# Inputs of a two-layer diffusion trunk laid out on the host: feature-major x, condition and vectors, weights in contiguous chunks

## The chip, the cores and the metric

The kernel runs on one core of a Trainium2 chip. The metric is the device time of one execution in microseconds (us); the median of three runs is shown. All data is f32.

## The reference, cut to what matters

The program runs two layers over two groups of tokens: 512 latent tokens (x_sample, conditioned by c) and 128 context tokens (x_prompt, conditioned by c_ctx). D_MODEL is 1024. What the change touches is the head of each layer:

```python
mod = (jax.nn.silu(cond) @ lw['w_ada'] + lw['b_ada'])[:, None, :]
sh1, sc1, gt1, sh2, sc2, gt2 = jnp.split(mod, 6, axis=-1)
h = rmsnorm(x, lw['g_norm1']) * (1.0 + sc1) + sh1
(qa, ka, va, qb, kb, vb, zb, ab, bb, qc, kc, vc, ga, gb, gc) = split_cols(h @ lw['w_in'])
```

w_ada is 1024 x 6144 and w_in 1024 x 8208 for each layer. The short convolution of the DeltaNet branch reads conv_w, its decays read the 16 columns ab and bb of w_in, and the expert router reads w_router. After the branches and the output projection comes the expert-choice mixture of 16 experts, which reads 96 chunks of 2 MB in each layer.

## The kernel before, in words

x is held in SBUF feature-major as xT, 128 partitions x 8 blocks k x 640 tokens (512 latent, then 128 context). h is held in the same way as hT. Weights pass through a ring of three slots of 2 MB (four in the expert stage). SyncE (SP) issues their loads in the order of PLAN: for a layer first the w_ada chunks 0 to 3, then the w_in chunks qb, kb, vb, zb, then the rest of w_ada and w_in mixed, the branch and output weights, and the experts (`load_plan`, the DMA itself in `load`). `slot_free` lets SP issue the load of a chunk once the chunk that was three before it has been used. A w_ada or w_in chunk is 512 columns of all 1024 rows, so a partition takes 8 pieces of 2 KB from 8 rows of the matrix. PE takes the chunks in the same order.

Start of the program. ScalarE (ACT) issues two loads of x as it lies, tokens on partitions, into xtok. GpSimd (POOL) issues the first constants, then c and c_ctx as 8 rows of 128 each into crow, then ten small loads of layer vectors into vrow, one row for each 128 values. PE turns crow (L1071), and DVE copies the result into ccol, padded with zeros, which is the stationary side of the w_ada matmuls. PE turns x_prompt (L1077) and x_sample (L1082) through PSUM, eight blocks of five tiles, and ACT copies each block out to xT (L1579, L1582) and squares it (L1598); DVE adds the squares (L2000). Between the blocks PE does the matmuls of w_ada chunk 0 (after block 3) and chunk 1 (after block 6), L957. Then PE sums the squares over the partitions (L1053 to L1057), does chunks 2 and 3, turns the vectors (L972), and folds the modulation (L966). ACT takes the root, DVE the reciprocal (L1991) and the vectors (L2011), ACT copies the modulation out (L1587, L1591), and DVE and ACT make hT block by block: `norm_scale` (L2006) and `shift` (L1619). The projection of qb starts on the context columns (L933, 64 matmuls; its first eight wait for a block of hT each) and goes on with the latent columns (L943). SP issues w_ada chunk 3 after chunk 0 is used, qb after chunk 1, kb after chunk 2, and vb after chunk 3.

Turn of the layers. After the experts PE does w_ada chunk 0 of the next layer (L957), then adds up the experts' output and turns it back to feature-major (L1528 to L1537) from ysum, which POOL loads from DRAM (L901, five loads of 512 KB), with w_ada chunks 1 to 3 between the blocks and the turn of the vectors after block 6. POOL issues the ten vector loads and the small loads (a_log, dt_bias, lam_qk, the 16 columns ab of w_in as wab, w_router) right behind the ysum loads.

Of the kernel before, what the change touches and what calls it, by code (L numbers as in the profile page):

```python
# [106 lines left out]
LAYER_CHUNKS = PRE_CHUNKS + NMOE  # L107
FIRST_UNITS = KD + 2

# [47 lines left out]
def wo_unit(l, half, m):  # L157

    return unit_no(l, "wo") + (8 + half if m is None else 4 * half + m)


def x_unit(k):
    return 2 + k

# [205 lines left out]
def build(nc, A, O):  # L370
    with ExitStack() as ctx:
# [32 lines left out]
        def at(off, shape):  # L404
            n = int(np.prod(shape))
            v = arena[:, off:off + n]
            if len(shape) == 2:
                v = v.rearrange("p (a b) -> p a b", a=shape[0])
            if len(shape) == 3:
                v = v.rearrange("p (a b c) -> p a b c", a=shape[0], b=shape[1])  # L410
            return v
# [68 lines left out]
        iota, onehot = at(9856, (T,)), at(9216, (T,))  # L480
        xtok = at(0, (NT, D))
        gates, gatep = at(15104, (512,)), at(15616, (256,))
        xrow = hT.rearrange("p k t -> p (k t)").rearrange("p (t d) -> p t d", t=NT)
        frow = at(10496, (D,))
        ysq = at(NS, (D,))
        crow = at(5120, (P,))

# [19 lines left out]
        def tile_t(t):  # L507
            return slice(t * P, (t + 1) * P)
# [49 lines left out]
        def _(sp):  # L558
# [8 lines left out]
            def load(c, src, words=4096, n=512):  # L567
                slot_free(c)
                s = slot_of(c)[0]
                sp.dma_start(ring[s][:, 0:words].rearrange("p (k n) -> p k n", n=n), src)\  # L570
                    .then_inc(sig[f"chunk{s}_loaded"], 16)

            for l in range(DEPTH):
                win = A["w_in"][l].rearrange("(k p) n -> p k n", p=P)

                def load_plan(q):
                    name, i = PLAN[q]
                    c = chunk_no(l, name, i)
                    if name == "ada":
                        load(c, A["w_ada"][l].rearrange("(k p) n -> p k n", p=P)[:, :, 512 * i:512 * i + 512])  # L580
                    elif name == "wo":
                        load(c, A["w_out"][l].rearrange("(k p) n -> p k n", p=P)[:, :, 512 * i:512 * i + 512])
                    elif name.startswith("br"):
                        load(c, A["w_br_" + name[2]][l].rearrange("(k p) n -> p k n", p=P)[:, :, 512 * i:512 * i + 512],
                             2048)
                    else:
                        load(c, win[:, :, SEG[name] + 512 * i:SEG[name] + 512 * i + 512])

# [117 lines left out]
        def _(pool):  # L706
            first = CST["tri"][0]
            pool.dma_start(cst[:, 0:first], A["consts"][:, 0:first]).then_inc(sig["consts_loaded"], 16)
            for i, n in enumerate(("c", "c_ctx")):
                src = A[n][0] if n == "c" else A[n]  # L710
                pool.dma_start(crow[8 * i:8 * i + 8, :], src.rearrange("(k p) -> k p", p=P))\
                    .then_inc(sig["cond_loaded"], 16)
            for l in range(DEPTH):

                if l:
                    pool.wait_ge(sig["logits_rowed"], 2 * l)
                rows = [(V_BADA, 48, A["b_ada"][l].rearrange("(m p) -> m p", p=P)),
                        (V_G1, 8, A["g_norm1"][l].rearrange("(m p) -> m p", p=P)),
                        (V_G2, 8, A["g_norm2"][l].rearrange("(m p) -> m p", p=P)),
                        (V_GO, 1, A["g_onorm"][l:l + 1, :]), (V_GS, 1, A["g_subln"][l:l + 1, :])]  # L720
                for r, n, src in rows:
                    pool.dma_start(vrow[r:r + n, :], src).then_inc(sig["vectors_loaded"], 16)
                for j in range(CONV):
                    pool.dma_start(vrow[V_CONV + 12 * j:V_CONV + 12 * j + 12, :],
                                   A["conv_w"][l, j].rearrange("(c p) -> c p", p=P)).then_inc(sig["vectors_loaded"], 16)
                if l == 0:
# [7 lines left out]
                    .then_inc(sig["small_loaded"], 16)  # L734
                pool.dma_start(wab, A["w_in"][l].rearrange("(k p) n -> p k n", p=P)[:, :, SEG["ab"]:SEG["ab"] + 16])\
                    .then_inc(sig["small_loaded"], 16)
                pool.dma_start(wrt, A["w_router"][l].rearrange("(k p) n -> p k n", p=P)).then_inc(sig["small_loaded"], 16)

# [44 lines left out]

                pool.wait_ge(sig["vectors_turned"], l + 1)
                pool.memset(rpt, 0.0).then_inc(sig["rows_cleared"], 1)
# [119 lines left out]
        def _(pe):  # L905
# [63 lines left out]

            def turn_vectors(l):  # L970
                pe.wait_ge(sig["vectors_loaded"], 160 * (l + 1))
                tr(W[3 if l else 2][:, 0:V_ROWS], vrow[0:V_ROWS, :], ident[0:V_ROWS, 0:V_ROWS])\  # L972
                    .then_inc(sig["vectors_turned"], 1)

            def modulate(l, a):
                for _ in ada(l, a):
                    pass
# [90 lines left out]
            pe.wait_ge(sig["consts_loaded"], 16)  # L1068
            pe.wait_ge(sig["cond_silu"], 1)
            pe.wait_ge(sig["cond_loaded"], 32)  # L1070
            tr(W[0][:, 0:16], crow[0:16, :], ident[0:16, 0:16]).then_inc(sig["cond_turned"], 1)  # L1071
            pe.wait_ge(sig["cond_ready"], 1)
            pe.wait_ge(sig["x_loaded"], 32)
            for half in range(2):
                big = begin(half)
                for k in range(4):
                    last = tr(big[:, tile_t(k)], xtok[:, NTS, tile_t(4 * half + k)], ident)  # L1077
                used(last)
            for k in range(KD):
                big = begin(x_unit(k))  # L1080
                for t in range(NTS):
                    last = tr(big[:, tile_t(t)], xtok[:, t, tile_t(k)], ident)  # L1082
                used(last)
                if k in (3, 6):
                    modulate(0, k // 4)
            norm_sum(0)
            modulate(0, 2)

            for l in range(DEPTH):
                if l == 0:  # L1090
                    modulate(0, 3)
                    turn_vectors(0)
                    for _ in fold(0, 3):
                        pass
# [437 lines left out]
                for k in range(KD):  # L1532
                    if k >= 1:
                        pe.wait_ge(sig["x_added"], XADDS * (l + 1) - KD + k - 1)
                    mm(W[2 + 2 * (k % 2)][:, :], final[:, tile_t(k)], onehot[0:SL, 0:TS], start=True, stop=False)
                    for t in range(NTS):
                        last = mm(W[2 + 2 * (k % 2)][:, tile_t(t)], ysum[t][:, tile_t(k)], ident,  # L1537
                                  start=False, stop=t == NTS - 1)
                    last.then_inc(sig["sum_turned"], 1)
                    if k in (1, 3, 5):  # L1540
                        modulate(l + 1, (k + 1) // 2)
                    if k == 6:
                        turn_vectors(l + 1)
                norm_sum(2 * l + 2)
# [17 lines left out]
        def _(act):  # L1562
# [3 lines left out]

            act.dma_start(xtok[:, 0:NTS, :], A["x_sample"][0].rearrange("(t p) d -> p t d", p=P))\
                .then_inc(sig["x_loaded"], 16)
            act.dma_start(xtok[:, NTS, :], A["x_prompt"][0]).then_inc(sig["x_loaded"], 16)

# [50 lines left out]

            act.wait_ge(sig["cond_loaded"], 32)
            a_(crow[0:16, :], crow[0:16, :], ACT.Silu).then_inc(sig["cond_silu"], 1)
            for half in range(2):
                copy_context(half, xT[:, 4 * half:4 * half + 4, TS:T])
            for k in range(KD):
                copy_unit(x_unit(k), xT[:, k, 0:TS])
                act.wait_ge(sig["unit_emptied"], x_unit(k) + 1)
                square(0, k)
# [347 lines left out]
        def _(dve):  # L1977
# [31 lines left out]
            def keep_vectors(l):  # L2009
                dve.wait_ge(sig["vectors_turned"], l + 1)  # L2010
                ch.link(v_.tensor_copy(vcol[:, :], W[3 if l else 2][:, 0:V_ROWS]))  # L2011

            v_.memset(ones[:, :], 1.0)
            v_.memset(small[:, 528:544], 0.0)
            v_.memset(W[5], 0.0)
            ch.link(v_.memset(ccol[:, :], 0.0))
            dve.wait_ge(sig["cond_turned"], 1)
            for g in range(2):
                last = v_.tensor_copy(ccol[:, 0:8 * KD].rearrange("p (k c) -> p k c", c=8)[:, :, 6 + g], W[0][:, KD * g:KD * g + KD])
            last.then_inc(sig["cond_ready"], 1)  # L2020
            dve.wait_ge(sig["consts_loaded"], 16)
# [500 lines left out]

            dve.wait_ge(sig["vectors_loaded"], 160 * DEPTH + 16)
            dve.wait_ge(sig["scattered"], 16 * SUMS * DEPTH)
# [14 lines left out]


# [15 lines left out]
```

## Time and profile before

| | us |
|---|---|
| median of 3 runs (lowest, highest) | 3163.93 (3163.28, 3166.62) |
| the profiled execution | 3165.57 |
| its span in the profile | 3163.8 |
| PE busy | 3071.8 (97%) |
| DVE busy | 1240.3 (39%) |
| ACT busy | 612.5 (19%) |
| POOL busy | 243.2 (8%) |

The span is cut into 40 slices of 79 us in the page's strips. PE is at nine tenths in nearly all of them; the DMA strip stands at nine tenths in two blocks of slices, which are the expert stages of the two layers, and between two and seven tenths elsewhere. Every time below is in us from the start of the span. The profiled execution lies 1.64 us above the median, and 1.8 us of it are outside the span.

### The profile page before, as it was taken

How to read it: one execution, taken by the hardware profiler on the slowest of the kernel's cores; microseconds unless marked ns; L12 is line 12 of the kernel's file. 1: busy time of each engine (PE TensorE's matmuls, PEld its weight loads, DVE VectorE, ACT ScalarE, POOL GpSimd, SP SyncE). 2: the span in 40 equal slices, each digit the busy share in tenths (PEclk: the TensorE clock that was granted, in tenths of full speed). 3: DMA queues.
4: the chain of work that ended last, by engine and by line, in shares of the span. 5: the costliest groups of instructions: out<-in, count | busy, mean ns of one | idle time of the engine just before them, and what ended most of it. 6: DMA issues, size and time to landing. Idle time of an engine off the chain costs nothing.

```text
span 3163.8 us, 43528 instructions
## 1 busy us (share of the span) xinstructions
PE 3071.8 (97%) x18861; PEld 1628.3 (51%) x18861; DVE 1240.3 (39%) x2402; ACT 612.5 (19%) x1358; POOL 243.2 (8%) x391
## 2 busy tenths in 40 slices
PE   7999999999998999999999999999999989999998
PEld 4555565656556444444355546665565464443433
DVE  4459553364343121121154694432644331121113
ACT  3141001143423000000022400011534230000001
POOL 1011000011001000000100100001110010000000
PEclk9999999999999999999999999999999989999999
DMA  7346543522333999999961573544224259999997
GB/s 243 110 127 187 151 140 98 162 92 72 130 126 128 347 393 388 394 391 387 386 194 61 176 193 96 150 140 123 79 72 157 97 179 369 394 395 389 391 390 291
DMA packets 227135, 695.17 MB, mean 220 GB/s; under 512 B 12210, under 2 KB 25750, under 8 KB 223616
## 3 DMA queue, kind: packets, MB, share of 16 engines
q1 hardware_dynamic: 199200, 613.97, 54.9%
q0 software_dynamic: 21312, 62.80, 6.8%
q10 hardware_dynamic: 6432, 15.62, 1.3%
q8 instruction: 149, 2.44, 0.3%
q14 instruction: 42, 0.34, 0.0%
HBM read 618.66 MB, written 73.68 MB: 219 GB/s over the span
## 4 chain that ended last, share of the span: by engine, by line
PE 91%; DMA 5%; ACT 2%; DVE 1%; issue 0%; SPq 0%; ACTq 0%; DVEq 0%
PE unit L994 14%; PE unit L1480 13%; PE unit L943 12%; PE work L1483 10%; PE work L1480 6%; PE unit L1006 4%; PE unit L985 4%; PE unit L1025 4%; PE unit L1352 3%; PE unit L933 3%; DMA ring<-in_w_e_gate 2%; PE unit L1305 1%; PE work L1173 1%; PE work L957 1%; PE unit L1364 1%; PE work L1196 1%
## 5 line engine op out<-in xcount | busy, mean ns | idle before, releaser
L994 PE MATMUL unit<-hT,ring 128*128 128x512 f32 x1024 | 452.6, 594 | 0.0
L1480 PE MATMUL unit<-ring,arena 128*64 128x512 f32 x1568 | 356.1, 600 | 5.3 <-DMA ring<-in_w_e_gate 3.9
L994 PEld LDWEIGHTS unit<-hT,ring 128*128 128x128 f32 x1024 | 189.4, 190 | 217.7 <-issue 217.7
L2486 DVE SCALAR_TENSOR_TENSOR arena<-work,arena 32x256 f32<-32x256 f32 x128 | 61.6, 482 | 552.1 <-PE work L1483 550.7
L1483 PE MATMUL work<-ring,arena 128*32 128x256 f32 x4608 | 274.8, 382 | 0.0
L1480 PEld LDWEIGHTS unit<-ring,arena 128*64 128x64 f32 x1568 | 109.9, 138 | 227.4 <-issue 216.0
L943 PE MATMUL unit<-hT,ring 128*128 128x512 f32 x512 | 222.2, 592 | 0.0
L1483 PEld LDWEIGHTS work<-ring,arena 128*32 128x32 f32 x4608 | 136.8, 109 | 159.5 <-issue 80.6
L1954 ACT ACTIVATE arena<-work 128x512 f32<-128x512 f32 x32 | 19.1, 597 | 849.9 <-PE work L1497 849.9
L1582 ACT ACTIVATE xT<-unit 128x512 f32<-128x512 f32 x100 | 59.5, 595 | 598.9 <-PE unit L994 393.0
L1480 PE MATMUL work<-ring,arena 128*64 128x512 f32 x736 | 166.6, 594 | 2.1 <-ACT arena L1955 2.1
L943 PE MATMUL unit<-arena,ring 128*128 128x512 f32 x384 | 166.8, 592 | 0.0
L943 PEld LDWEIGHTS unit<-hT,ring 128*128 128x128 f32 x512 | 96.2, 190 | 115.8 <-issue 115.3
L1006 PE MATMUL unit<-ring,hT 128*128 128x512 f32 x320 | 140.7, 594 | 0.0
L985 PEld LDWEIGHTS unit<-hT,ring 128*128 128x128 f32 x1024 | 116.8, 192 | 12.4 <-issue 12.4
L985 PE MATMUL unit<-hT,ring 128*128 128x128 f32 x1024 | 121.2, 277 | 0.0
L896 POOL DMA_INDIRECT moe_sum<-arena,slotu x30 | 42.8, 1427 | 993.6 <-DVE arena L2491 930.7
L1025 PE MATMUL unit<-hT,ring 128*128 128x512 f32 x256 | 117.0, 600 | 0.0
L943 PEld LDWEIGHTS unit<-arena,ring 128*128 128x128 f32 x384 | 72.0, 190 | 86.1 <-issue 86.1
L2214 DVE TENSOR_TENSOR arena<-arena,work 32x512 f32<-32x512 f32 x60 | 41.0, 683 | 186.9 <-PE work L1196 186.5
L1352 PE MATMUL unit<-arena,ring 128*128 128x512 f32 x256 | 110.7, 593 | 0.0
L2470 DVE TENSOR_TENSOR arena<-work,amod 128x256 f32<-128x256 f32 (+1 forms) x128 | 36.8, 349 | 187.2 <-PE work L1449 187.2
(435 smaller groups left out, 4026.6 us busy)
## 6 DMA issues: line engine op xcount, KB each, us to landing
ring<-in_w_e_gate SPq DMA_DIRECT2D x50, 2048.0 KB, 16.1
ring<-in_w_e_up SPq DMA_DIRECT2D x48, 2048.0 KB, 13.5
ring<-in_w_e_down SPq DMA_DIRECT2D x46, 2048.0 KB, 15.2
ring<-in_w_in SPq DMA_DIRECT2D x32, 2048.0 KB, 18.1
ring<-in_w_ada SPq DMA_DIRECT2D x24, 2048.0 KB, 8.8
arena<-in_w_e_down SPq DMA_DIRECT2D x18, 2048.0 KB, 14.9
arena<-in_w_e_up SPq DMA_DIRECT2D x16, 2048.0 KB, 13.5
arena<-in_w_e_gate SPq DMA_DIRECT2D x14, 2048.0 KB, 16.2
```

Source lines behind the costliest of these rows:

```text
L896: pool.indirect_dma_start(moesum[l], bass.IndirectOffsetOnAxis(token[:, s:s + 1], 0), Y[s % NROWS][0:SL, :], None, compute_op=ALU.add)\
L933: last = mm(bank[:, tile_t(m)], w[:, k, m * P:(m + 1) * P], src[:, k, TS:T], start=k == 0, stop=k == kk - 1)
L943: last = mm(bank[:, :], w[:, k, m * P:(m + 1) * P], src[:, k, 0:TS], start=k == 0, stop=k == kk - 1)
L985: last = mm(bank[:, tile_t(m)], w[:, k, m * P:(m + 1) * P], hT[:, k, TS:T], start=k == 0, stop=k == KD - 1)
L994: last = mm(bank[:, :], w[:, k, m * P:(m + 1) * P], hT[:, k, 0:TS], start=k == 0, stop=k == KD - 1)
L1006: last = mm(big[:, :], hT[:, k, tile_t(t)], w[:, k, :], start=k == 0, stop=k == KD - 1)
L1025: last = mm(ps[1][:, :], w[:, s, (j - 1) * P:j * P], hT[:, s, 0:TS], start=s == 0, stop=s == KD - 1)
L1352: last = mm(bank[:, :], wo[half][:, k, m * P:(m + 1) * P], merged[:, k, 0:TS], start=k == 0, stop=k == KD - 1)
L1480: last = mm(big[SLS * c:SLS * c + SLS, :], x, w[:, kk, 512 * c:512 * c + 512], start=k == 0, stop=k == KD - 1)
L1483: last = mm(low[SLOTP * c:SLOTP * c + SLOTP, 0:256], xp, w[:, kk, 256 * c:256 * c + 256], start=k == 0, stop=k == KD - 1)
L1582: emptied(a_(dst, unit(n)[:, :], f, scale=scale))
L2486: STT(y[SLS:SLS + SLOTP, 256 * c:256 * c + 256], W[5][r, 0:256], gpro[r, e:e + 1], gatep[r, :], ALU.mult, ALU.mult)
```

## The change

The host lays the inputs out before the launch. x comes as one array of 128 partitions x 8 x 640, so that xT is loaded in place in two halves of 1.25 MB; c and c_ctx come as 128 x 2 x 8, and the layer vectors as 128 x 126, already turned. The chunks of w_ada and w_in come as 128 partitions x 8 x 512 each, 16 KB contiguous for a partition and 2 MB for a chunk, and the 16 columns ab and w_router as 128 x 8 x 16. In the kernel the turns of x, of the condition and of the vectors go, with the ten PSUM units of the first; the silu of the condition is written straight into ccol by ACT, and the vectors are copied by DVE from vrow to vcol. The order of PE at the start becomes: w_ada chunks 0 and 1, sum of squares, chunks 2 and 3, fold.

```diff
-FIRST_UNITS = KD + 2
+FIRST_UNITS = 0
...
                     if name == "ada":
-                        load(c, A["w_ada"][l].rearrange("(k p) n -> p k n", p=P)[:, :, 512 * i:512 * i + 512])
+                        load(c, A["w_ada"][l, i])
...
-                        load(c, win[:, :, SEG[name] + 512 * i:SEG[name] + 512 * i + 512])
+                        load(c, A["w_in"][l, (SEG[name] - 16 * (SEG[name] > SEG["ab"])) // 512 + i])
...
-            for i, n in enumerate(("c", "c_ctx")):
-                src = A[n][0] if n == "c" else A[n]
-                pool.dma_start(crow[8 * i:8 * i + 8, :], src.rearrange("(k p) -> k p", p=P))\
-                    .then_inc(sig["cond_loaded"], 16)
+            pool.dma_start(cond, A["cond"]).then_inc(sig["cond_loaded"], 16)
...
-                for r, n, src in rows:
-                    pool.dma_start(vrow[r:r + n, :], src).then_inc(sig["vectors_loaded"], 16)
-                for j in range(CONV):
-                    pool.dma_start(vrow[V_CONV + 12 * j:V_CONV + 12 * j + 12, :],
-                                   A["conv_w"][l, j].rearrange("(c p) -> c p", p=P)).then_inc(sig["vectors_loaded"], 16)
+                pool.dma_start(vrow[:, 0:V_ROWS], A["vectors"][l]).then_inc(sig["vectors_loaded"], 16)
...
-                pool.dma_start(wab, A["w_in"][l].rearrange("(k p) n -> p k n", p=P)[:, :, SEG["ab"]:SEG["ab"] + 16])\
+                pool.dma_start(wab, A["w_ab"][l])\
...
-                pool.dma_start(wrt, A["w_router"][l].rearrange("(k p) n -> p k n", p=P)).then_inc(sig["small_loaded"], 16)
+                pool.dma_start(wrt, A["w_router"][l]).then_inc(sig["small_loaded"], 16)
...
             pe.wait_ge(sig["consts_loaded"], 16)
-            pe.wait_ge(sig["cond_silu"], 1)
-            pe.wait_ge(sig["cond_loaded"], 32)
-            tr(W[0][:, 0:16], crow[0:16, :], ident[0:16, 0:16]).then_inc(sig["cond_turned"], 1)
             pe.wait_ge(sig["cond_ready"], 1)
-            pe.wait_ge(sig["x_loaded"], 32)
-            for half in range(2):
-                big = begin(half)
-                for k in range(4):
-                    last = tr(big[:, tile_t(k)], xtok[:, NTS, tile_t(4 * half + k)], ident)
-                used(last)
-            for k in range(KD):
-                big = begin(x_unit(k))
-                for t in range(NTS):
-                    last = tr(big[:, tile_t(t)], xtok[:, t, tile_t(k)], ident)
-                used(last)
-                if k in (3, 6):
-                    modulate(0, k // 4)
+            modulate(0, 0)
+            modulate(0, 1)
             norm_sum(0)
             modulate(0, 2)
...
-            act.dma_start(xtok[:, 0:NTS, :], A["x_sample"][0].rearrange("(t p) d -> p t d", p=P))\
-                .then_inc(sig["x_loaded"], 16)
-            act.dma_start(xtok[:, NTS, :], A["x_prompt"][0]).then_inc(sig["x_loaded"], 16)
+            for half in range(2):
+                act.dma_start(xT[:, 4 * half:4 * half + 4, :], A["x"][:, 4 * half:4 * half + 4, :])\
+                    .then_inc(sig[f"x{half}_loaded"], 16)
...
-            act.wait_ge(sig["cond_loaded"], 32)
-            a_(crow[0:16, :], crow[0:16, :], ACT.Silu).then_inc(sig["cond_silu"], 1)
-            for half in range(2):
-                copy_context(half, xT[:, 4 * half:4 * half + 4, TS:T])
+            act.wait_ge(sig["cond_loaded"], 16)
+            act.wait_ge(sig["cond_cleared"], 1)
+            for g in range(2):
+                last = a_(ccol[:, 0:8 * KD].rearrange("p (k c) -> p k c", c=8)[:, :, 6 + g], cond[:, g, :], ACT.Silu)
+            last.then_inc(sig["cond_ready"], 1)
             for k in range(KD):
-                copy_unit(x_unit(k), xT[:, k, 0:TS])
-                act.wait_ge(sig["unit_emptied"], x_unit(k) + 1)
+                if k % 4 == 0:
+                    act.wait_ge(sig[f"x{k // 4}_loaded"], 16)
                 square(0, k)
...
             def keep_vectors(l):
-                dve.wait_ge(sig["vectors_turned"], l + 1)
-                ch.link(v_.tensor_copy(vcol[:, :], W[3 if l else 2][:, 0:V_ROWS]))
+                dve.wait_ge(sig["vectors_loaded"], 16 * (l + 1))
+                v_.tensor_copy(vcol[:, :], vrow[:, 0:V_ROWS]).then_inc(sig["vectors_kept"], 1)
+                dve.wait_ge(sig["vectors_kept"], l + 1)
...
+    def chunks(w, n):
+        return w.reshape(DEPTH, w.shape[1] // P, P, n, 512).transpose(0, 3, 2, 1, 4)
...
+    w, ab = a.pop("w_in"), SEG["ab"]
+    out["w_in"] = chunks(np.concatenate([w[:, :, :ab], w[:, :, ab + 16:]], 2), 16)
...
+    out["w_ada"] = chunks(a.pop("w_ada"), 12)
+    rows = np.concatenate([a.pop("x_sample")[0], a.pop("x_prompt")[0]], 0)
+    out["x"] = rows.T.reshape(KD, P, T).transpose(1, 0, 2)
```

## Rows read from the trace of the kernel before

**Rows 1.** The page: span, and busy time of the engines.
```profile
span 3163.8 us, 43528 instructions
PE 3071.8 (97%) x18861; PEld 1628.3 (51%) x18861; DVE 1240.3 (39%) x2402; ACT 612.5 (19%) x1358; POOL 243.2 (8%) x391
```

**Rows 2.** Waits of PE: what for, us in total, times, longest.
```profile
PE unit L933 <- DMA ring<-in_w_in: 5.9, 1, 5.9
PE unit L1480 <- DMA ring<-in_w_e_gate: 3.9, 4, 1.6
PE work L957 <- DMA ring<-in_w_ada: 3.2, 1, 3.2
```

**Rows 3.** Chain of waits: start, us, what; the last row is a later projection.
```profile
1.28 13.91 DMA arena<-in_x_prompt
...
26.99 15.17 DMA ring<-in_w_in
...
42.20 10.17 PE unit L933 x64
...
79.83 7.14 PE unit L933 x64
```

**Rows 4.** Stretches: length, busy by engine (instructions), PE clock, DMA share, GB/s.
```profile
10.00:15.00 5.00, 0.00 (x0) 0.00 (x0) 0.00 (x0) 0.00 (x0) 0.00 (x0) 1.00 1.03 386
25.00:30.00 5.00, 3.94 (x26) 1.66 (x26) 2.48 (x3) 4.89 (x8) 0.00 (x0) 1.00 1.05 387
33.00:41.00 8.00, 2.87 (x25) 1.33 (x17) 7.34 (x15) 4.26 (x12) 0.00 (x0) 0.80 1.01 175
42.00:49.20 7.20, 7.00 (x38) 7.00 (x39) 3.65 (x9) 3.34 (x6) 0.00 (x0) 0.58 1.04 371
118.00:120.00 2.00, 2.00 (x21) 2.00 (x20) 1.34 (x2) 0.00 (x0) 0.00 (x0) 1.00 1.05 410
153.00:155.00 2.00, 2.00 (x21) 2.00 (x20) 0.95 (x2) 0.00 (x0) 0.00 (x0) 1.00 1.03 239
```

**Rows 5.** Timeline of the start: start, us, engine, line, operation, idle before.
```profile
8.23 0.31 ACT L1623 ACTIVATE arena<-arena 16x128 f32<-16x128 f32 x1 [4.99 <-DMA arena<-in_c_ctx]
...
26.44 0.83 DVE L2000 TENSOR_TENSOR arena<-arena 128x640 f32<-128x640 f32 x1 [0.43 <-ACT arena L1598]
...
28.18 0.74 ACT L1598 ACTIVATE arena<-xT 128x640 f32<-128x640 f32 x1
...
31.44 4.34 DVE L1991 RECIPROCAL arena<-arena 128x128 f32<-128x128 f32 x2 [2.92 <-ACT arena L1603]
...
32.33 0.11 PEld L957 LDWEIGHTS work<-ring,ccol 128*8 128x8 f32 x4 [0.42 <-DMA ring<-in_w_ada]
...
34.62 0.60 ACT L1587 ACTIVATE arena<-work 128x512 f32<-128x512 f32 x1 [2.63 <-PE work L957]
...
37.48 7.86 ACT L1619 ACTIVATE hT<-hT,mod 128x128 f32<-128x128 f32 x16 [0.92 <-DVE hT L2006]
```

**Rows 6.** DMA issues of the first 130 us: KB each, us to landing.
```profile
cst<-in_consts POOLq DMA_DIRECT2D x1, 72.5 KB, 5.7
```

**Rows 7.** Stretches again, for PE's clock; columns as in rows 4.
```profile
37.50:38.00 0.50, 0.00 (x0) 0.00 (x0) 0.50 (x3) 0.50 (x2) 0.00 (x0) 0.77 1.18 147
42.10:43.00 0.90, 0.80 (x4) 0.80 (x4) 0.90 (x2) 0.90 (x2) 0.00 (x0) 0.50 1.05 398
1575.00:1579.00 4.00, 0.78 (x8) 0.12 (x8) 1.50 (x2) 0.00 (x0) 0.00 (x0) 1.00 1.08 367
1611.00:1612.00 1.00, 0.59 (x3) 0.62 (x4) 1.00 (x5) 1.00 (x4) 0.00 (x0) 0.66 1.02 317
```

**Rows 8.** Chain of waits at the turn of the layers: the projection there.
```profile
1611.41 8.97 PE unit L933 x64
```

**Rows 9.** Timeline of the turn of the layers; columns as in rows 5.
```profile
1578.68 1.90 PE L957 MATMUL work<-ring,ccol 128*8 128x512 f32 x16 [3.22 <-DMA ring<-in_w_ada]
...
1602.55 0.27 PE L972 MATMUL work<-cst,vrow 126*128 126x126 f32 x1
```

More of the change, by code:

```diff
@@ L159, in wo_unit @@
     return unit_no(l, "wo") + (8 + half if m is None else 4 * half + m)
-def x_unit(k):
-    return 2 + k
 def chunk_no(l, name, i=0):
@@ L480, in build @@
         iota, onehot = at(9856, (T,)), at(9216, (T,))
-        xtok = at(0, (NT, D))
         gates, gatep = at(15104, (512,)), at(15616, (256,))
@@ L485, in build @@
         ysq = at(NS, (D,))
-        crow = at(5120, (P,))
+        cond = at(5120, (2, KD))
         ps = [ctx.enter_context(nc.psum_tensor(f"unit{i}", [P, 512], F32)) for i in range(2)]
@@ L573, in _ @@
             for l in range(DEPTH):
-                win = A["w_in"][l].rearrange("(k p) n -> p k n", p=P)
                 def load_plan(q):
@@ L716, in _ @@
                     pool.wait_ge(sig["logits_rowed"], 2 * l)
[L717 to L720, printed above, removed]
-                for r, n, src in rows:
-                    pool.dma_start(vrow[r:r + n, :], src).then_inc(sig["vectors_loaded"], 16)
-                for j in range(CONV):
-                    pool.dma_start(vrow[V_CONV + 12 * j:V_CONV + 12 * j + 12, :],
-                                   A["conv_w"][l, j].rearrange("(c p) -> c p", p=P)).then_inc(sig["vectors_loaded"], 16)
+                pool.dma_start(vrow[:, 0:V_ROWS], A["vectors"][l]).then_inc(sig["vectors_loaded"], 16)
                 if l == 0:
@@ L782, in _ @@
                 load_lower(1)
-                pool.wait_ge(sig["vectors_turned"], l + 1)
+                pool.wait_ge(sig["vectors_kept"], l + 1)
                 pool.memset(rpt, 0.0).then_inc(sig["rows_cleared"], 1)
@@ L968, in fold @@
                 yield
[L970 to L973, printed above, removed]
             def modulate(l, a):
@@ L1091, in _ @@
                     modulate(0, 3)
-                    turn_vectors(0)
                     for _ in fold(0, 3):
@@ L1541, in _ @@
                         modulate(l + 1, (k + 1) // 2)
-                    if k == 6:
-                        turn_vectors(l + 1)
                 norm_sum(2 * l + 2)
@@ L2015, in _ @@
             v_.memset(W[5], 0.0)
[L2016 to L2020, printed above, removed]
+            v_.memset(ccol[:, :], 0.0).then_inc(sig["cond_cleared"], 1)
             dve.wait_ge(sig["consts_loaded"], 16)
@@ L2521, in finish @@
                 STT(ysum[t], ysum[t], orms[:, t:t + 1], frow, ALU.mult, ALU.mult).then_inc(sig["y_ready"], 1)
-            dve.wait_ge(sig["vectors_loaded"], 160 * DEPTH + 16)
+            dve.wait_ge(sig["vectors_loaded"], 16 * DEPTH + 16)
             dve.wait_ge(sig["scattered"], 16 * SUMS * DEPTH)
@@ L2538, with laid_out, columns_of @@
          ("new_na_v", (1, DEPTH, TP, H, P)), ("new_state_delta", (1, DEPTH, 2, H, P, P))]
+def laid_out(inputs):
+    a = {name: np.asarray(x) for name, x in inputs.items()}
+    out = {}
+    def chunks(w, n):
+        return w.reshape(DEPTH, w.shape[1] // P, P, n, 512).transpose(0, 3, 2, 1, 4)
+    def columns_of(v):
+        return v.reshape(DEPTH, -1, P).transpose(0, 2, 1)
+    w, ab = a.pop("w_in"), SEG["ab"]
+    out["w_in"] = chunks(np.concatenate([w[:, :, :ab], w[:, :, ab + 16:]], 2), 16)
+    out["w_ab"] = w[:, :, ab:ab + 16].reshape(DEPTH, KD, P, 16).transpose(0, 2, 1, 3)
+    out["w_router"] = a.pop("w_router").reshape(DEPTH, KD, P, NE).transpose(0, 2, 1, 3)
+    out["w_ada"] = chunks(a.pop("w_ada"), 12)
+    rows = np.concatenate([a.pop("x_sample")[0], a.pop("x_prompt")[0]], 0)
+    out["x"] = rows.T.reshape(KD, P, T).transpose(1, 0, 2)
+    out["cond"] = np.stack([a.pop("c")[0], a.pop("c_ctx").reshape(D)]).reshape(2, KD, P).transpose(2, 0, 1)
+    out["vectors"] = np.concatenate([columns_of(a.pop(n)) for n in ("b_ada", "g_norm1", "g_norm2", "conv_w", "g_onorm", "g_subln")], 2)
+    return {**a, **out, "consts": constants()}
 def kernel(**inputs):
@@ L2546 @@
     arrays, A, O = {}, {}, {}
-    for name, a in list(inputs.items()) + [("consts", constants())]:
+    for name, a in laid_out(inputs).items():
         a = np.ascontiguousarray(a)
```

## The prediction

> **What bounds the kernel now.** I read the page first: PE is busy 3071.8 of 3163.8 us [rows 1], so whatever is gained must come from the 92 us in which PE stands, or from PE's own work. The waits of PE come next. Of those that end on a DMA, three bear on weights: 5.9 us for the first w_in chunk, 3.2 us for w_ada at the turn of the layers, and 3.9 us in four waits for expert weights [rows 2]. The expert loads aren't changed, and no other w_in or w_ada load is waited for: a projection of latents and context takes some 35 us of PE, a load 5 to 10 us. So making some 50 other loads shorter is worth nothing, and the two places are the start and the turn.
>
> The chain of waits shows what sets the start: x lands at 15.19, PE and ACT turn it, PE finishes w_ada chunk 1 at 26.97, only then qb's load is issued, and it takes 15.17 us to land; PE starts the qb projection at 42.20 [rows 3]. The stretches say why it takes so long. The DMA engines are full from the first microseconds (386 and 387 GB/s); w_ada and x take all of it. Behind them qb goes at 175 GB/s with the engines as busy, and a w_in chunk alone at 239, where a w_ada chunk alone, with pieces of 2 KB too, has 410 [rows 4].
>
> **The start, step by step.** What is removed from PE (turns of x, condition and vectors) and ACT (ten copies) lies before w_ada chunk 3, and that is bound by bytes: PE waited for it, and it is there at 32.33 [rows 5]. Ahead of and with it go 8.39 MB of w_ada, 2.62 MB of x and 0.14 MB of constants and vectors: 11.15 MB at 387 GB/s are 28.8 us, which leaves 3.5 us of the 32.3 seen for the first byte and the report of the end together (I split it, an estimate, in 2.7 and 0.8). The same bytes are loaded after the change, so chunk 3 lands at 32.3 again, as long as the queue never runs dry: chunk 3 must be issued before chunk 2's last byte, at (2.62 + 6.29 + 0.07) MB / 387 GB/s + 2.7 = 25.9. With x and weights sharing evenly until x lands at 15.2, chunk 0 lands near 15.7, its matmuls take 1.90 [rows 9], or up to 3.8 at half clock, and chunk 3 goes out at 17.6 to 19.5. Chunk 1 lands near 21.5, and qb goes out at 23.4 to 25.3 instead of 26.99, while the queue is still full until 31.5. Chunk 2 lands near 26.9.
>
> The condition is no bound. Now 8 KB over 128 partitions, it is priced by the constants, 128 partitions and 5.7 us [rows 6]: issued at 2.0, there by 7.7 to 8, as before [rows 5], and the two silus (below 0.31 each) are done by 8.6, 7 us before chunk 0. The vectors, one load of 63 KB, are in by 9 and needed at 36.
>
> The norm leaves the path. Eight squares of 0.74 and six adds of 0.83 [rows 5] follow the two halves of x, at 9 and 15.2: the last ends near 19, 9.9 us before the 28.92 of now. PE's sum comes behind chunk 1, at 23.4, and the reciprocals (4.34, now until 35.78) end near 31 to 32. The chain that is left is the modulation: chunk 3 at 32.33, ACT copies at 34.62, first block of hT begun at 37.48 and done at 37.97 [rows 5]. The turn of the vectors (0.3) stands beside ACT's copy; the copy of the vectors (0.3) on DVE now falls before the modulation is there. So the first block of hT is at 38.0, as now.
>
> Then qb. Its bytes follow chunk 3's: 2.10 MB at 387 GB/s are 5.4 us, so it lands at 32.3 + 5.4 = 37.7. Contiguous chunks aren't in the trace; the ends are the isolated 239 GB/s, 8.8 us and 41.1, and 410, 5.1 us and 37.4. I take 387, since w_ada's and x's different shapes run at it side by side. PE begins at 38.0 and not 42.2: 4.2 us.
>
> The length of the first projection changes too. It took 10.17 where a later one takes 7.14 [rows 3], since PE had stood for 5.9 us and its granted clock was 0.50, the lower of its two levels (1.2 of 2.4 GHz), when it began [rows 7]. After the change it resembles the one of the second layer, which starts as soon as hT does: 8.97 [rows 8], with 0.66 granted at its start. Between 8.97 and 10.17 I take 9.5, for PE's sparser start. 38.0 + 9.5 = 47.5 against 52.37: the start gives **4.9 us**.
>
> **PE's clock before that.** PE will work in pieces of 2 us with pauses up to 4 us, where it now works almost without a pause from 15.3. At the turn of the layers a pause of 3.2 us after steady work left the granted clock at 1.00 [rows 7], but at 37.5 it fell after 1.2 us of pause and some thin work before. If it is low when chunk 3 lands, the sixteen matmuls cost 1.9 more and the fold some 1.1 more: 3.0 of the 4.9. I take no loss, since chunk 1, sum and chunk 2 fill 21.5 to 28.8 nearly without a pause, and keep 3.0 as a bound.
>
> **The turn of the layers.** The w_ada chunk 0 is 3.22 us late there [rows 9]. Its queue holds the same bytes, but the loads of wab and w_router, 2048 pieces of 64 B, become 256 of 512 B, and nine small loads go, so that POOL issues the rest sooner, in the shade of the last expert. In that wait the rate is 367 GB/s [rows 7] against 387 [rows 4]: over 4 us that is 0.08 MB or 0.2 us. With what comes from the earlier issue I take 0.7 us, from 0 to 3.2, the whole wait (the ysum loads, 2.6 MB in the same seconds, must also be in, which makes 1.9 a likelier top). The turn L972 goes: 0.27 us long, mostly beside the next matmul [rows 9], I count 0.1. Sum 0.8.
>
> **Sum.** 4.9 + 0.8 = 5.7 us from the profiled 3165.57 is 3159.9; the profiled execution lies 1.64 above the median, so the median goes from 3163.93 to **3158.2**. Rest at nothing: x loads issued by ACT, two as before; ysum, spills, experts unchanged; the first w_in loads of the second layer land before 1611.41 already, where hT is waited for.
>
> **A rule against part of this.** The w_in rows lie 32832 B apart, 64 B off any larger boundary. The Trainium skill, page "DMA: Bandwidth & Descriptors", section "How a descriptor splits into AXI transactions", says that a piece that doesn't start on 256 B takes one transaction more, here nine instead of eight. If that were the whole gain of the new layout, w_in would go from 239 to some 269 GB/s, and not to 387. The trace speaks against it: from 42.0 to 49.2, when mostly kb's load is in flight, with the same row distance and offsets, the engines move 371 GB/s [rows 4]. So slowness belongs to some chunks' addresses rather than to alignment, and the contiguous w_ada and w_in have no such row distance. The loss could yet come back at new addresses.
>
> **Rivals.**
> - *w_in stays slow* (its rate isn't cured by layout). At 239 GB/s qb lands at 41.1, PE stands nearly as long and the first projection takes 10.17: the start gives 1.1, in all 1.9, 3162.0. For it: nobody has shown the cause. Against: kb, above.
> - *The clock is low at chunk 3.* 4.9 - 3.0 + 0.8 = 2.7, 3161.2. For it: the pause of up to 3.5 us before chunk 3 if PE keeps up. Against: the turn of the layers.
> - *Long pieces go faster, and ahead of others.* At 410 GB/s the 11.15 MB take 27.2, 1.6 sooner, and at the turn w_ada's 16 KB pieces overtake the 4 KB pieces of ysum, 1.9 in place of 0.7. 5.7 + 1.6 + 1.2 = 8.5, 3155.4. For it: 410 alone. Against: 386 to 387 through the whole start, whatever is mixed.
> - *Small loads starve behind long pieces: slower.* On each of 16 engines the constants and the condition are 16 pieces. If each waits for one piece of w_ada and one of x, 26 KB at 24 GB/s is 1.1 us a piece, and the condition is there at 20; PE then does chunk 0 at 20 and chunk 3 still goes out before 25.9. If it is two pieces of each, it is there at 37: chunk 3 goes out at 39, lands at 46, and the projection begins near 52, 9.6 later than now: with 0.8 back 3172.7. From a condition at 24 on each microsecond costs one, and from 29 on the kernel is slower than now. Against: x and weights share evenly at 4 KB to 2 KB pieces. The Trainium skill, same page, section "Queues, rings and completion order", says that an engine changes between queues at packets, not at bytes; the even share of now doesn't contradict it, and no run here shows 16 KB pieces.
>
> **Chances.** Forecast 0.62 (3156.5 to 3160.5 is its own range), w_in slow 0.10, clock 0.14, faster 0.10, starved 0.04. Low end 3155.0, just under the third rival, high end 3164.0, over the first two; the starved case and noise stay out. This kernel's measurement can't tell less than 0.2%, 6.3 us. Faster than that: all of the third rival, and a third of the forecast's (5.7 is near the line) gives 0.31. Slower: 0.04 and 0.01 for what I don't see. The rest, 0.64, is no change that can be measured.
>
> **What would show it.** The first L933 begins at 38.0 and released by hT, not by DMA; chunk 3 at 32.3; the isolated w_in chunk near 149 at over 350 GB/s; the last square before 20; the wait for w_ada at the turn below 3 us. A wait for in_w_in of over 2 us at the first L933 makes the first rival right, matmuls of chunk 3 that take 3.8 us the second, chunk 3 before 31 the third, a first L957 after 20 the fourth. Any difference in the expert stages or between 60 and 1550 us would be against my whole reading.

## The result

The changed kernel takes 3168.29 us (median of 20 runs, 3163.05 to 3179.09) where the kernel before takes 3165.56 in the same series (20 runs, 3160.61 to 3169.27). The ratio is 1.0015, 95% interval 1.0009 to 1.0021: slower, by 2.7 us in the medians and by 4.7 by the ratio, and not 5.7 faster. The profiled execution of the changed kernel took 3173.34 us (span 3171.2), 5 above its median, so the terms below add up to more than the medians differ by.

The waits of PE after the change (what for, us in total, times, longest):

```profile
PE work L940 <- DMA ring<-in_w_ada: 18.5, 3, 12.8
PE work L1491 <- DMA arena<-moe_sum: 14.7, 1, 14.7
PE work L1412 <- DMA arena<-h_rows,slotu: 8.6, 2, 5.0
PE unit L1443 <- DMA ring<-in_w_e_gate: 3.3, 3, 1.2
```

Two of the three waits of [rows 2] are gone, that for in_w_in and that for w_ada at the turn of the layers: the three for w_ada are now all at the start, in place of the one for x (6.4 us before). New is the second row: 14.7 us for moe_sum, the DRAM tensor that the ysum loads read.

The chain of waits at the start and at the turn (start, us, what), which answers to [rows 3] and [rows 8]; L916 is L933 of before:

```profile
16.48 13.81 DMA ring<-in_w_ada
...
35.72 10.31 PE unit L916 x64
...
73.49 7.14 PE unit L916 x64
...
1558.14 27.21 DMA arena<-moe_sum
1619.11 8.87 PE unit L916 x64
```

The first projection begins at 35.72, not 42.20, and ends at 46.03 instead of 52.37: 6.3 us gained, and still there when the experts of the first layer end. Then the chain goes through one load of ysum that took 27.21 us to land, and the second layer begins at 1619.11 instead of 1611.41.

The timeline of the changed kernel at the turn (start, us, engine, line, operation, idle before); L940, L884 and L1491 are L957, L901 and L1528 of before:

```profile
1549.83 21.36 SPq L565 DMA_DIRECT2D ring<-in_w_ada  x4
...
1555.92 2.79 POOL L884 DMA_DIRECT2D arena<-moe_sum  x5 [7.60 <-DMA moe_sum<-arena,slotu]
...
1568.89 1.90 PE L940 MATMUL work<-ring,ccol 128*8 128x512 f32 x16
...
1585.49 0.77 PE L1491 MATMUL work<-cst,arena 128*128 128x128 f32 x2 [14.69 <-DMA arena<-moe_sum]
```

w_ada chunk 0 is there in time (in [rows 9] PE waits 3.22 us for it). The five ysum loads are issued from 1555.92 on, 13 us before chunk 0 is used, and hold PE until 1585.49. In the kernel before PE came to this point at 1580.52 and did not wait.

Two stretches after the change (length; busy of PE, PEld, DVE, ACT, POOL; PE clock, DMA share, GB/s):

```profile
1575.00:1580.00 5.00, 0.00 (x0) 0.00 (x0) 0.00 (x0) 0.00 (x0) 0.00 (x0) 0.50 1.02 427
1585.00:1590.00 5.00, 4.51 (x21) 4.54 (x22) 0.72 (x4) 0.00 (x0) 0.00 (x0) 0.50 0.01 3
```

While PE stands, the DMA engines are full and move 427 GB/s, but mostly other data. The queues in the same 5 us (packets, MB, share of the 16 engines; q1 is SP's queue with w_ada, q0 POOL's with ysum and the small loads behind it):

```profile
q1 hardware_dynamic: 111, 1.77, 83.7%
q0 software_dynamic: 110, 0.36, 18.2%
```

The two queues have the same number of packets, but a w_ada piece is four times as long as one of ysum. In the kernel before, from 1570 to 1575, the packets are as even, and it is ysum that has the longer pieces and two thirds of the bytes:

```profile
q0 software_dynamic: 348, 1.25, 63.4%
q1 hardware_dynamic: 354, 0.72, 38.2%
```

The packets are not even in every stretch (from 1560 to 1575 after the change POOL's queue has 490 to 311 of SP's). And when PE goes on (the second stretch above), its granted clock is 0.50, the lower level, so that from L1491 to the first projection 33.6 us pass (1585.49 to 1619.11), where they were 30.9 (1580.52 to 1611.41).

So the profiled executions add up thus: start -6.3; w_ada's wait gone -3.2; wait for ysum +14.7; low clock after it +2.7; what is left, expert stages and the rest, -0.5. That is +7.4, from 3163.8 to 3171.2.

### The profile page after: what moved, and what is told of

Same layout as the page of the kernel before. It is cut to its first block, busy times and chain, and to the rows that moved or that the text cites. A ratio compares the mean times of both kernels' runs of the same rounds, so it can differ in the third digit from the quotient of the medians.

```text
span 3171.2 us, 43405 instructions
## 1 busy us (share of the span) xinstructions
PE 3068.7 (97%) x18818; PEld 1628.7 (51%) x18818; DVE 1238.6 (39%) x2400; ACT 606.2 (19%) x1349; POOL 231.3 (7%) x372
## 4 chain that ended last, share of the span: by engine, by line
PE 91%; DMA 5%; ACT 2%; DVE 1%; issue 0%; SPq 0%; POOL 0%; ACTq 0%; DVEq 0%; POOLq 0%
PE unit L972 14%; PE unit L1443 13%; PE unit L926 12%; PE work L1446 10%; PE work L1443 7%; PE unit L984 4%; PE unit L963 4%; PE unit L1003 4%; PE unit L1315 3%; PE unit L916 3%; DMA ring<-in_w_e_gate 2%; PE work L940 1%; PE unit L1268 1%; PE work L1136 1%; PE unit L1327 1%; PE work L1159 1%
## 5 line engine op out<-in xcount | busy, mean ns | idle before, releaser
L1443 PE MATMUL unit<-arena 128*64 128x512 f32 x480 | 109.6, 599 | 0.0
```

The costliest lines, as they stand in the source:

```text
L1443: last = mm(big[SLS * c:SLS * c + SLS, :], x, w[:, kk, 512 * c:512 * c + 512], start=k == 0, stop=k == KD - 1)
```

## The experiments

Theory S, formed on the trace after: a DMA engine takes turns between queues by pieces, so w_ada's pieces of 16 KB on SP's queue push back the ysum loads, whose pieces are 4 KB, on POOL's queue. Its rivals: the ysum loads are late for their own reasons (C); the contiguous chunks or their higher rate do it, not the length of a piece (B); POOL's queue is the weak one (Q). "Before" is run beside each series on the same chip: medians 3164.07 in the first (e1 to e4), 3165.59 in the second (e5 to e8), 3164.57 in the third.

### e1: w_ada of the second layer in rows again

```diff
-                        load(c, A["w_ada"][l, i])
+                        if l:
+                            load(c, A["w_ada_rows"].rearrange("(k p) n -> p k n", p=P)[:, :, 512 * i:512 * i + 512])
+                        else:
+                            load(c, A["w_ada"][l, i])
```

> The changed kernel, but the w_ada chunks of the second layer are read as before, from row-major w_ada in pieces of 2 KB. Theory S (long w_ada pieces on SP's queue hold back the 4 KB pieces of the five ysum loads on POOL's queue at the turn of the layers): the last ysum load lands within 15 us instead of 27.2, PE's wait of 14.7 us for it is gone or below 2 us, the first projection of layer 1 begins some 36 us after the experts' end instead of 50, and the start's gain of 6.4 us is left: 3159 us against 3165.6 before and 3168.3 changed. Rival C (the scatters into the same DRAM rows or the expert loads make ysum late, whatever w_ada's pieces are): ysum lands after 27 us again and the time stays at 3168.

Measured: 3154.8 us, ratio 0.9972 (0.9962 to 0.9981) to before. The five ysum loads from issue to landing:

```profile
DMA to landing us min/median/max: 7.3/10.2/14.0
```

The same view of the changed kernel as it is:

```profile
DMA to landing us min/median/max: 10.6/17.5/27.2
```

The edit puts back all twelve w_ada chunks of the second layer; four of them are loaded at the turn. PE no longer waits for ysum. The chain of e1 at the turn:

```profile
1548.51 21.23 DMA ring<-in_w_ada_rows
1602.40 7.80 PE unit L919 x64
```

The median is some 13 us below that of the changed kernel. That is S, and against C. It came out 4 us better than I expected: I had counted on the start alone, but at the turn PE also waits only 0.52 us for w_ada chunk 0, in pieces of 2 KB as before, where it waited 3.22 before. So in this execution most of that wait went without long pieces; with e3 below, where it is 2.92, it doesn't show that the other parts of the change remove it every time.

### e2: ysum first

```diff
                 for q in range(8):
+                    if l and q == 1:
+                        sp.wait_ge(sig["scattered"], 16 * SUMS * l)
                     load_plan(q)
```

> The changed kernel with one wait more: SP issues w_ada chunk 1 of the second layer only when the five ysum loads have landed. Theory S: with only one w_ada chunk and the last expert chunk ahead of them, the ysum loads land within 14 us of their issue, about when PE is through with w_ada chunk 0; chunk 1 goes out then and lands 6 to 8 us later, just before PE wants it; the wait of 14.7 us shrinks to below 3 us, and the time is 3158 to 3161 us. Rival C (ysum is late for a reason other than w_ada's pieces): the wait stays at 14 us, w_ada chunks 1 to 3 come later still, and the time is above 3170.

Measured: **3153.39 us**, ratio 0.9964 (0.9951 to 0.9977) to before: the fastest version measured, with e1 close behind (their intervals overlap), and 5 us better than expected. The ysum loads, then the timeline of SP and PE:

```profile
DMA to landing us min/median/max: 6.6/8.3/12.4
```

```profile
1567.42 1.90 PE L942 MATMUL work<-ring,ccol 128*8 128x512 f32 x16
...
1569.12 1.29 SPq L565 DMA_DIRECT2D ring<-in_w_ada  x3
1569.25 0.49 PE L1493 MATMUL work<-cst,arena 128*128 128x128 f32 x2
```

The last ysum load lands as PE ends chunk 0, and the three held w_ada loads go out then; PE waits 0.2 us for one, and the second layer's first projection begins at 1600.34. The layout is the changed kernel's: what went is the loss that long pieces ahead of ysum made.

### e3, e9, e6: pieces of 2, 4 and 8 KB, chunks contiguous all the same

The edit, for 2 KB (g = 1; g = 2 and 4 for the others):

```diff
-                        load(c, A["w_ada"][l, i])
+                        load(c, A["w_ada"][l, i].rearrange("k p n -> p k n"), n=512 * g)
...
+    def pieces(w, n):
+        return w.reshape(DEPTH, KD // g, g, P, n, 512).transpose(0, 4, 1, 3, 2, 5).reshape(DEPTH, n, KD // g, P, 512 * g)
```

and the same for w_in.

> The changed kernel with w_ada and w_in chunks still contiguous, 2 MB each, but with k outermost inside a chunk, so that a partition takes eight pieces of 2 KB, 256 KB apart. Theory S (length of a piece sets the share of a queue): ysum lands within 15 us, x at the start within 15 us instead of 20.7, and the time is 3159 to 3161. Rival B (the contiguous chunk itself, its higher rate, crowds the other queue): ysum at 27 us and 3168 again. It also parts two causes of w_in's slowness and of the start's higher rate: if the distance between rows made w_in slow, an isolated w_in chunk now runs at over 350 GB/s; if the piece length did, it stays at 240. If piece length made the start run at 430 GB/s instead of 387, the start falls back to 387 and the first projection begins at 38, not 35.7.

> The changed kernel with w_ada and w_in in four pieces of 4 KB for a partition and chunk, as long as the pieces of ysum. By the runs so far the last ysum load lands after 14.1 us beside 2 KB, 22.9 beside 8 KB and 27.2 beside 16 KB. If the share goes by piece length, it is an even one here: last landing at 16 to 19 us, PE's wait 1 to 6 us, and the time between that of 2 KB (3159.5) and that of 8 KB (3165.9), 3157 to 3163. If 4 KB pieces give the start its higher rate (420 and more, as 8 and 16 KB do), the first projection begins below 37.5; if 387, at 37.9 as with 2 KB.

> The changed kernel with w_ada and w_in in two pieces of 8 KB for a partition and chunk. If the share of a queue goes by the length of its piece (4 KB of ysum to 8 KB, a third, against a fifth at 16 KB and two thirds at 2 KB), the last ysum load lands between the 14 us of 2 KB and the 27 us of 16 KB, at 17 to 21 us, PE waits 2 to 7 us for it, and the time is 3155 to 3162. If only pieces above some length crowd the others, it is as with 2 KB or as with 16 KB. The start: 420 to 430 GB/s as with 16 KB, or 387 as with 2 KB, if there the number of pieces decides.

Measured, with the changed kernel in the last row (the medians are from three series; x is the median landing of its two halves; the rate is that of 10 to 25 us; all but the medians and ratios from one profiled execution each):

| pieces | median us | ratio to before (95%) | last ysum load | PE waits for ysum | x lands after | GB/s at the start | first projection at |
|---|---|---|---|---|---|---|---|
| 2 KB | 3159.5 | 0.9987 (0.9979 to 0.9996) | 14.1 | none | 9.1 | 385 | 37.9 |
| 4 KB | 3161.4 | 0.9995 (0.9986 to 1.0004) | 16.8 | 2.8 | 9.5 | 411 | 36.2 |
| 8 KB | 3165.9 | 1.0003 (0.9994 to 1.0012) | 22.9 | 10.2 | 11.6 | 423 | 36.9 |
| 16 KB | 3168.3 | 1.0015 (1.0009 to 1.0021) | 27.2 | 14.7 | 15.8 | 425 | 35.7 |

Four points in one line: the longer the piece, the later its neighbours, at both ends of the program, and with contiguous chunks in all four, so B falls. The row of 2 KB is from the fastest execution of its twelve, 5.8 us below their median, and that of 8 KB from one 2.3 above; with 2 KB PE waits 2.9 us for w_ada chunk 0 at the turn instead. The waits of PE with pieces of 8 KB, then of 4 KB:

```profile
PE work L1491 <- DMA arena<-moe_sum: 10.2, 1, 10.2
```

```profile
PE work L1491 <- DMA arena<-moe_sum: 2.8, 1, 2.8
```

Length has a use too: the rate of the start rises with it from 385 to 425 GB/s. For 8 KB I expected 17 to 21 us of landing and 3162 at most; it is worse, nearer to 16 KB.

The same kernels narrow down why w_in was slow. In the changed kernel, with 16 KB, an isolated w_in chunk goes at 426 GB/s (146 to 148). An isolated w_in chunk with contiguous pieces of 2 KB (columns as in [rows 4]):

```profile
146.00:148.00 2.00, 2.00 (x20) 2.00 (x19) 1.93 (x3) 0.49 (x2) 0.00 (x0) 1.00 1.00 358
148.00:150.00 2.00, 2.00 (x20) 2.00 (x19) 0.24 (x1) 0.00 (x0) 0.00 (x0) 1.00 1.04 393
```

against the same chunk read from rows, in e4 below:

```profile
152.00:154.00 2.00, 2.00 (x20) 2.00 (x19) 1.93 (x3) 0.60 (x2) 0.00 (x0) 1.00 0.96 229
154.00:156.00 2.00, 2.00 (x20) 2.00 (x19) 0.35 (x1) 0.00 (x0) 0.00 (x0) 1.00 1.02 249
```

Pieces are 2 KB in both: the addresses of w_in's rows made it slow. Alignment by itself doesn't explain it (kb, [rows 4]); whether it is the distance between rows was not tried apart.

### e4: x, condition and vectors laid out, the weights as before

```diff
-                        load(c, A["w_ada"][l, i])
+                        load(c, A["w_ada"][l].rearrange("(k p) n -> p k n", p=P)[:, :, 512 * i:512 * i + 512])
-                        load(c, A["w_in"][l, (SEG[name] - 16 * (SEG[name] > SEG["ab"])) // 512 + i])
+                        load(c, A["w_in"][l].rearrange("(k p) n -> p k n", p=P)[:, :, SEG[name] + 512 * i:SEG[name] + 512 * i + 512])
```

> The changed kernel with w_ada and w_in as before (row-major, pieces of 2 KB); x, condition, vectors, wab and w_router stay laid out. Theory S: nothing is held back at the turn (ysum within 15 us, PE waits up to 3 us for w_ada chunk 0), and the start gains only what the earlier issue of qb's load gives, since qb is still read at some 200 GB/s: first projection at about 41 instead of 42.2, and 3164 to 3165 us. Rival X (laying out x is worth most of the 6.4 us of the start): first projection at 38 or before and 3160.

Measured: 3163.03 us, ratio 0.9998 (0.9990 to 1.0007): no change. The first projection begins at 43.09, where I expected about 41. That part by itself gives nothing that can be measured, and shows a second thing: PE, with no turns of x to do, comes to w_ada chunk 3 at the lower clock. Its matmuls in e4 and then the stretch:

```profile
31.83 3.60 PE L940 MATMUL work<-ring,ccol 128*8 128x512 f32 x16 [3.33 <-DMA ring<-in_w_ada]
```

```profile
32.00:36.00 4.00, 3.43 (x16) 0.31 (x8) 0.00 (x0) 0.50 (x1) 0.00 (x0) 0.50 1.02 184
```

3.60 instead of 1.90: my second rival's mechanism, real here, and hidden by qb's slow load (184 GB/s). In the changed kernel chunk 3 takes 1.90 at the full clock.

### e5: the kernel before, with 16 KB pieces of w_ada in the second layer

```diff
-                        load(c, A["w_ada"][l].rearrange("(k p) n -> p k n", p=P)[:, :, 512 * i:512 * i + 512])
+                        if l:
+                            load(c, A["w_ada1"][i])
+                        else:
+                            load(c, A["w_ada"][l].rearrange("(k p) n -> p k n", p=P)[:, :, 512 * i:512 * i + 512])
...
+    inputs["w_ada1"] = np.asarray(inputs["w_ada"])[1].reshape(KD, P, 12, 512).transpose(2, 1, 0, 3)
```

> The kernel before with one part of the change alone: the w_ada chunks of the second layer are contiguous, 16 KB for a partition; all else as before. Theory S: the start is as before (first projection at 42), the last ysum load lands after 22 us or more instead of 14.3, PE waits for it some 8 to 13 us, and the time is 3164 + 5 to 12, that is 3169 to 3176. A rival, that the loss at the turn needs the other parts of the change too (earlier small loads, vectors in one load): 3164 or below.

Measured: 3179.29 us, ratio 1.0040 (1.0027 to 1.0054). Its wait and the ysum loads:

```profile
PE work L1531 <- DMA arena<-moe_sum: 13.7, 1, 13.7
```

```profile
DMA to landing us min/median/max: 8.4/16.9/26.5
```

The loss can be put into the old kernel by this one edit: the median is 13.7 us above that of before. The wait and the low clock after it are a little more than that, and w_ada's wait at the turn is gone, as in the changed kernel. The time is above my range (3176).

### e7: ysum issued by ACT

```diff
-                    pool.dma_start(ysum[NTS - t], moesum[l][tile_t(NTS - t), :]).then_inc(sig["scattered"], 16)
+                    act.dma_start(ysum[NTS - t], moesum[l][tile_t(NTS - t), :]).then_inc(sig["sums_back"], 16)
...
```

The waits on these loads go over to the new semaphore with them.

> The changed kernel with the five ysum loads issued by ACT on its queue and not by POOL. Theory S (piece length): they are held back just the same, the last lands after 22 to 28 us, the time is 3165 to 3170. Rival Q (it is POOL's queue that gives way, not the short piece): they land within 15 us, and the time is 3153 to 3158.

Measured: 3171.26 us, ratio 1.0015 (1.0006 to 1.0024). The loads, on ACT's queue:

```profile
DMA to landing us min/median/max: 8.8/18.5/27.4
```

As from POOL, and PE waits 15.7 us. Q falls: ACT's queue gives way as POOL's does. The time is 1.3 us above my range (3170).

### e8: the weights' part of the change alone

x, condition and vectors as in the kernel before, w_ada and w_in as in the changed one (and the columns ab in an array of their own, since w_in no longer holds them).

> The weights' part of the change alone: w_ada and w_in contiguous in pieces of 16 KB, while x comes token-major in pieces of 4 KB and is turned on PE, and condition and vectors come as before. Theory S: beside 16 KB pieces x gets a fifth of the rate and lands at 25 to 32 us instead of 15.2, the first projection begins at 45 to 52 instead of 42.2, and the turn of the layers loses its 5 to 14 us too: 3172 to 3185. If the share doesn't go by piece length, x lands near 15 and the first projection at 38: 3160 to 3168.

Measured: 3184.05 us, ratio 1.0056 (1.0042 to 1.0070). The chain of the start:

```profile
1.26 24.30 DMA arena<-in_x_prompt
...
48.40 10.17 PE unit L932 x64
```

Beside 16 KB, x in pieces of 4 KB lands at 25.56 instead of 15.19 [rows 3], and 6.2 us are lost at the start as well. The queues from 8 to 11 us (q10 is ACT's, with x) have the same number of packets and bytes as 3 to 1:

```profile
q1 hardware_dynamic: 75, 0.97, 77.3%
q10 hardware_dynamic: 75, 0.31, 25.2%
```

So the laid-out x, worth nothing alone (e4), is worth some 13 us to the first projection once the weights come in long pieces (48.40 against 35.72).

### e10: the changed kernel again

> The changed kernel as it is, a second time, beside the 4 KB one. Its first profiled execution took 3173.3 us while its median is 3168.3. If the wait for the ysum loads (14.7 us there) is what varies from execution to execution, a profiled execution nearer to the median shows a shorter wait; if it is 14 to 15 again whatever the time, the variation comes from elsewhere, such as the expert stages. Median 3166 to 3171, start (first projection) at 35.7 within 0.3 in either case.

Measured: 3169.99 us, ratio 1.0013 (1.0004 to 1.0022), first projection at 35.45, wait for ysum 15.0 us. But this profiled execution took 3173.18, the longest of its eleven, as the first had been long, so it doesn't tell whether the wait is shorter in the executions of 3165. One thing that varies is seen across the traces: from the end of the first 64 matmuls of L916 (L933 before) to the point where PE wants w_ada chunk 0 of the second layer, 1523.1 us pass in the kernel before and 1522.9 in the changed one, but 1518.2 in e3, 1519.2 in e7 and 1523.7 in e1, with no order by kernel. What else varies stays open.

## Why the prediction was wrong, point by point

- **The start: right, and sized too small.** I took 4.9 us, measured 6.3 in the profile. First projection not at 38.0 but at 35.72. The term that was off is the rate: I put 11.15 MB at 387 GB/s; with 16 KB pieces it is 425, and chunk 3 is used at 30.33 and not at 32.33. The third rival had named this (410), and its sign, chunk 3 before 31, came true. The landings of x in between, 9 and 15.2 "with x and weights sharing evenly", were wrong by the very effect that decides the turn: the halves land at 12.9 and 20.7, and the last square ends at 24.0, not before 20. It cost nothing there: the reciprocals ended at 31.7, and the modulation was there at 34.3. The length of the first projection was 10.31, not 9.5: PE began it at the lower clock.
- **qb's load, right in its rate, and close.** It came at full rate behind chunk 3: the first block of hT was done at 35.6, and the first weight load of the projection went through at 35.68. The profile puts the last 1.76 us before that weight load down to in_w_in and PE's own wait down to hT, so both ended within 0.1 us. The first rival is dead for contiguous chunks.
- **The turn of the layers: the step that failed.** I gave it -0.7 us with bounds from 0 to 3.2 of gain, and no price below nothing. I noted that "the ysum loads, 2.6 MB in the same seconds, must also be in", and that 16 KB pieces might "overtake the 4 KB pieces of ysum", and booked that as a gain for w_ada, capped at 1.9. I never asked what the overtaken load would then cost: 14.7 us of waiting and 2.7 of low clock, against 3.2 gained. With turns piece by piece, one of 4 KB to one of 16 KB, ysum has a fifth of 387 GB/s, 77 GB/s, and its 2.62 MB take 34 us: an estimate, and an upper one, since the long loads end before it. Measured: 27.2, where 14.3 was enough before.
- **The slower rival: the right mechanism at the wrong place.** "Small loads starve behind long pieces" was given 0.04 and tied to the condition at the start. The condition came at 10.3 instead of 8.2, harmless as worked out. Who starves is whoever shares the engines with w_ada and is waited for next: at the turn that is ysum. And what I held against this rival, that x and weights "share evenly at 4 KB to 2 KB pieces", was misread. In the kernel before, from 8 to 11 us, they do so by packets and not by bytes:

```profile
q10 hardware_dynamic: 183, 0.75, 63.5%
q1 hardware_dynamic: 189, 0.39, 35.8%
```

x, with pieces of twice the length, has twice the bytes of w_ada. This was in the trace before the prediction, and it spoke for the rival.
- **What the page said.** The Trainium skill, page "DMA: Bandwidth & Descriptors", section "Queues, rings and completion order", says that an engine goes round the queues at packet boundaries. The runs agree in kind: two queues at work have nearly equal numbers of packets in several stretches (183 to 189, 75 to 75, 111 to 110), and the last ysum load came later with the length of its neighbour's pieces, in four steps from 14.1 to 27.2 us. How many packets an engine takes at a turn these counts can't tell. I set that sentence aside for want of a run; it was the one that spoke against the change.
- **Nothing else moved.** The stretch between the first projection and the turn took 1522.9 us and 1523.1 before, though 50 loads of w_ada and w_in became shorter: so far my reading of the waits held. That the two agree so closely is in part luck, since the same stretch differs by up to 5.5 us between the traces (e10).

## What to carry to other kernels

A layout that makes one stream's pieces longer takes bandwidth from every other stream that is in flight with it. Before lengthening pieces, list for each such load the shorter-pieced loads beside it and who waits for them, and read packets and bytes by queue where two are in flight: equal packets with unequal bytes tell beforehand which will lose; if one is on the path, lengthen its pieces too (as x here), or hold the long loads back until it has landed, one semaphore wait that turned 3168 us into 3153 here.

## What the runs showed of the hardware

- Loads beside longer pieces on another queue came later: ysum at 4 KB on POOL's queue, last landing 14.1, 16.8, 22.9 and 27.2 us beside w_ada of 2, 4, 8 and 16 KB on SP's; 27.4 from ACT's queue beside 16 KB.
- Two busy queues had nearly the same number of packets, one piece each, in several stretches, and so bytes by piece length: 0.75 to 0.39 MB at 4 to 2 KB, 0.31 to 0.97 MB at 4 to 16 KB. At the turn of the changed kernel it was 490 to 311 packets.
- The rate of the loads at the start rose with piece length at full queues: 385, 411, 423, 425 GB/s for weights in 2, 4, 8 and 16 KB, one execution each.
- A w_in chunk out of rows 32832 B apart came at 229 to 249 GB/s, the same pieces of 2 KB out of a contiguous 2 MB block at 358 to 393.
- After a pause of 14.7 us PE worked at the lower clock (0.50 granted), and the way to the next projection took 2.7 us more.
